# The first modulation of a two-block transformer kernel, made in eight chunks of channels

## What is computed

```
for i in range(DEPTH):
    mod = (silu_c @ ada_w[i] + ada_b[i])[:, None, :]
    mod_c = (silu_cc @ ada_w[i] + ada_b[i])[None, None, :]
    sh_m, sc_m, g_m, sh_f, sc_f, g_f = jnp.split(mod, 6, axis=-1)
    h = modulate(rmsnorm(x, norm_mix_w[i]), sh_m, sc_m)          # h * (1 + scale) + shift
    hc = modulate(rmsnorm(ctx, norm_mix_w[i]), shc_m, scc_m)
    y, y_c = ab_mixer(h, hc, ab_w_in[j], ...)                    # p = h @ w_in, 2560 columns
k = (mem @ w_k); v = (mem @ w_v)                                 # second block, needed late
```

## Time and profile before

| | us |
|---|---|
| median of 3 runs (2553.43 to 2554.41) | 2553.57 |
| the profiled execution, whole | 2553.91 |
| its span (first to last instruction) | 2552.1 |
| TensorE busy in the span | 2494.1 (98%) |
| VectorE busy | 1990.8 (78%) |
| ScalarE busy | 1175.3 (46%) |

### The profile page before, as it was taken

How to read it: one execution, slowest core, us unless ns; L and a number is a source line. 1 busy time by engine, 2 the same in 40 slices (tenths; PEclk the granted TensorE clock), 3 DMA queues, 4 the chain that set the end, 5 groups by cost and what they waited for, 6 DMA issues and landing times.

```text
span 2552.1 us, 41954 instructions
## 1 busy us (share of the span) xinstructions
PE 2494.1 (98%) x16459; PEld 2142.8 (84%) x16459; DVE 1990.8 (78%) x2455; ACT 1175.3 (46%) x1498; POOL 88.1 (3%) x116
## 2 busy tenths in 40 slices
PE   7999999999999999999999899999999999999998
PEld 5877788888889998889999688888888888888886
DVE  3876877777767886758887747888888888889887
ACT  3436200001421005531014737777777777777776
POOL 0100100000000001000002000000000000000000
PEclk9999999999999999999999999999999999999999
DMA  8843454443335454334545025999899999999996
GB/s 334 320 161 131 165 174 167 165 172 116 116 108 219 181 181 141 108 108 170 184 175 197 18 100 207 373 364 375 334 375 363 361 346 374 366 350 359 363 374 251
DMA packets 91398, 602.75 MB, mean 236 GB/s; under 512 B 9840, under 2 KB 12912, under 8 KB 24688
## 3 DMA queue, kind: packets, MB, share of 16 engines
q1 hardware_dynamic: 76848, 540.05, 56.0%
q0 software_dynamic: 14400, 60.56, 6.7%
HBM read 598.47 MB, written 2.10 MB: 235 GB/s over the span
## 4 chain that ended last, share of the span: by engine, by line
PE 92%; DVE 5%; ACT 2%; SPq 1%; issue 1%; DMA 1%; DVEq 0%; ACTq 0%
PE bank L1195 12%; PE bank L1198 12%; PE bank L1199 12%; PE bank L2546 8%; PE bank L2550 8%; PE bank L2549 8%; PE bank L2577 4%; PE bank L2581 4%; PE bank L2580 4%; PE bank L542 2%; PE bank L1432 1%; PE bank L1453 1%; PE bank L1443 1%; PE bank L2559 1%; PE bank L1244 1%; PE bank L1245 1%
## 5 line engine op out<-in xcount | busy, mean ns | idle before, releaser
L991 DVE TENSOR_TENSOR ring_part<-ring,arena_part 128x2048 fp32r<-128x2048 f32 x481 | 1080.2, 2275 | 33.1 <-ACT arena_part L1010 15.9
L2902 ACT ACTIVATE arena_part<-ring 128x2048 fp32r<-128x2048 f32 x339 | 647.7, 1920 | 191.0 <-DMA ring<-in_stream 190.1
L1195 PE MATMUL bank<-arena_part 128*128 128x256 f32 (+1 forms) x2040 | 650.3, 319 | 8.3 <-DVE ring_part L991 8.3
L1199 PE MATMUL bank<-arena_part,ring_part 128*128 128x256 f32 (+1 forms) x2040 | 646.7, 317 | 0.0
L1198 PE MATMUL bank<-h_part,arena_part 128*128 128x256 f32 (+1 forms) x1496 | 474.2, 317 | 0.0
L1195 PEld LDWEIGHTS bank<-arena_part 128*128 128x128 f32 x2040 | 388.6, 190 | 39.0 <-issue 12.6
L1199 PEld LDWEIGHTS bank<-arena_part,ring_part 128*128 128x128 f32 x2040 | 388.6, 190 | 25.7
L2546 PE MATMUL bank<-arena_part,h_part 128*128 128x512 f32 x896 | 354.1, 395 | 0.0
L2550 PE MATMUL bank<-arena_part,h_part 128*128 128x512 f32 x896 | 349.6, 390 | 0.0
L2549 PE MATMUL bank<-ring_part,h_part 128*128 128x512 f32 x896 | 348.9, 389 | 0.0
L1299 ACT ACTIVATE arena<-bank 128x256 f32<-128x256 f32 (+1 forms) x66 | 30.1, 455 | 636.7 <-PE bank L1199 635.8
(11 more groups left out here) (378 smaller groups left out, 3077.3 us busy)
## 6 DMA issues: line engine op xcount, KB each, us to landing
ring<-in_stream SPq DMA_DIRECT2D x511, 1024.0 KB, 4.9
arena<-in_ada_stream POOLq DMA_DIRECT2D x80, 512.0 KB, 4.6
consts<-in_mem_w POOLq DMA_DIRECT2D x8, 512.0 KB, 4.1
consts<-in_small POOLq DMA_DIRECT2D x1, 2800.0 KB, 11.8
arena<-in_c_rows POOLq DMA_DIRECT2D x2, 1024.0 KB, 8.3
arena<-in_ab_bias POOLq DMA_DIRECT2D x1, 2048.0 KB, 8.6
arena<-in_t_bias POOLq DMA_DIRECT2D x1, 2048.0 KB, 7.9
arena<-in_mem_t SPq DMA_DIRECT2D x1, 1024.0 KB, 5.0
```

The lines of the kernel that those rows point to most:

```text
L991: return nc.vector.tensor_tensor(low, value, high.bitcast(F32), ALU.subtract)
L1195: m = nc.tensor.matmul(out_ap, w_high, high, start=start, stop=False)
L1199: return nc.tensor.matmul(out_ap, w_low, high, start=False, stop=stop)
L2902: nc.scalar.activation(high, ring[:, where], ACT.Copy).then_inc(sem("moe_high"), 1)
```

## The change

The 2048 columns of `ada_w` now come as eight slots of their own (`ada_mix`), cut by output: slot c holds shift and scale of channel chunk c, for all input rows. They are no part of the ring's count any more and go to the ring places 0, 1, 2, 0, 1, 2, 3, 2. AB0 and AB1 are loaded ahead of them, and rounded ahead of the row copies. TensorE makes slot c in eight matmuls of 256 columns (L1958, four strips of 32 rows in PSUM), ScalarE copies the strips (L2723), two small matmuls add the strips and turn them into columns (`fold_rows`, L1968), and VectorE makes shift and scale of this chunk (`first_scale`, L3164 and L3168). The norm of chunk c, its split, and the products of AB0 and AB1 with it (`first_products`, L2002 to L2010, four banks) follow at once, while later slots of `ada_mix` still come in. SiLU of `c_rows`, the rounding of AB2 and AB3, and two of the 24 sums stand inside the loop over chunks. Memory keys and values use other banks, 18 filler matmuls stand ahead of the first value products, and GpSimd clears a buffer for the wider `silu_c`.

```diff
-START = ["K0a", "A0", "A1", "K0b", "A2", "A3", "V0a", "A4", "A5", "V0b", "A6", "A7"]
+START = ["K0a", "K0b", "V0a", "V0b"]
...
@@ TensorE
-            for k in range(2):
-                ada_products(k)
...
+            mem_key_products(range(2, 4))
+            warm(18)
+            mem_value_products()
...
+            ada_products(0)
+            ada_products(1)
             mem_value_products()
+            fold_rows(0)
             rstd_pe(bk, TT)
-            turn_rows()
-            split_products(bk, w, 4, ab_high, h_part, TT, ab_slot_high, sides=2)
+            fold_rows(1)
+            ada_products(2)
...
+            for c in range(DC):
+                if c + 3 < DC:
+                    ada_products(c + 3)
+                if c + 2 < DC:
+                    fold_rows(c + 2)
+                first_products(c)
@@ ScalarE
+            for c in range(DC):
+                for s in range(2):
+                    t = slice(SEQ * s, SEQ * (s + 1))
+                    scaled_act(bk, c == DC - 1 and s == 1, spread_last)
+                    nc.scalar.activation(ab_high[:, c, t], hv[:, c, t], ACT.Identity, bias=shift(0, 0, c, s))\
+                        .then_inc(sem("in_high"), 1)
+                if c + 3 < DC:
+                    copy_rows(c + 3)
+                if c == 1:
+                    silu_rows(rows_first, 1)
+                if c in (3, 5):
+                    slot_high_act(bk, AB_AT + 2 + (c == 5), ab_slot_high, fresh=True)
@@ VectorE
+            first_scale(0)
             spread = spread_dve(bk)
...
+            for c in range(DC):
...
+                if c + 1 < DC:
+                    first_scale(c + 1)
...
+                if c in (4, 6):
+                    slot_low_dve(bk, AB_AT + 2 + (c == 6), ab_slot_high)
+                elif c in (3, 5):
+                    if c == 3:
+                        dve.wait_ge(sem("c_rows_ready"), 1)
+                    first_chunks(c // 2 - 1, c // 2)
...
-            for n in range(2, 7):
-                first_chunks(3 * n - 6, 3 * n - 3)
+            for n, chunks in ((4, (2, 6)), (5, (6, 10)), (6, (10, 13))):
+                first_chunks(*chunks)
                 slot_low_dve(bk, AB_AT + n, ab_slot_high)
...
-            first_chunks(15, 18)
+            first_chunks(13, 15)
             slot_low_dve(bk, AB_AT + 7, ab_slot_high)
-            first_chunks(18, 21)
+            first_chunks(15, 19)
...
-            first_chunks(21, 24)
+            first_chunks(19, 22)
+            for c in range(2, 4):
+                to(kT[:, c, :])
+            slot_low_dve(bk, AB_AT + 9, ab_slot_high)
+            first_chunks(22, 24)
@@ SyncE
+            for c in range(3):
+                sp.wait_ge(sem("slots_used"), c + 2)
+                load_ada(c)
+            for c in range(3, 6):
+                sp.wait_ge(*marks["ada_made"][c - 3])
+                load_ada(c)
...
+            load_ada(6)
+            for n in range(RING, RING + 2):
+                sp.wait_ge(*marks["ada_made"][n - RING + 3])
+                load(n)
+            sp.wait_ge(*marks["ada_made"][5])
+            load_ada(7)
```

More of the change, by code:

```diff
@@ L50 @@
     ("sinks", 8), ("expert_id", EXPERTS), ("cmp_row_ok", 2),
-    ("slot_id", P), ("earlier", P), ("fold", 32),
+    ("slot_id", P), ("earlier", P),
 ]
@@ L63 @@
 LN_EVENTS = 6 * DC
-SLOTS_ADA = 16 * DC // TILES
 ADA_FIRST = [(0, n) for n in range(16, 40)]
@@ L110, in leave, with build @@
         self.i = None
-def build(nc, stream, ada_stream, mem_w, c_rows, small, x_t, ctx_t, mem_t, ab_bias, sgu, t5_bias, band_bias, cmp_bias, out):
+def build(nc, stream, ada_mix, ada_stream, mem_w, c_rows, small, x_t, ctx_t, mem_t, ab_bias, sgu, t5_bias, band_bias, cmp_bias, out):
     with ExitStack() as ctx:
@@ L1932, in _, with ada_products, fold_rows @@
             pe.wait_ge(sem("silu_c_ready"), 1)
[L1934 to L1945, removed]
-            for k in range(2):
-                ada_products(k)
             pe.wait_ge(sem("mem_split"), DC)
             mem_key_products(range(2, 4))
-            ada_products(2)
+            warm(18)
+            mem_value_products()
+            rows_copied, ada_made = [], []
+            marks["ada_made"] = ada_made
+            def ada_products(c):
+                b = bk.fill(ADA_BANKS[c % 2])
+                rows_copied.append(bk.freed(bk.turn - 1))
+                pe.wait_ge(free(b), bk.emptied())
+                at, room, landed = ada_at(c)
+                pe.wait_ge(sem(f"ada_landed{at}"), landed)
+                for late in range(2):
+                    for g in range(4):
+                        k = 4 * late + g
+                        m = nc.tensor.matmul(PS[b][32 * g:32 * g + 32, X2], silu_c[:, k, :],
+                                             room[:, k * SEQ:(k + 1) * SEQ], start=not late, stop=bool(late))
+                m.then_inc(full(b), 1)
+                ada_made.append((full(b), bk.filled()))
+            def fold_rows(c):
+                pe.wait_ge(*rows_copied[c])
+                b = bk.fill(FOLD_BANK)
+                pe.wait_ge(free(b), bk.emptied())
+                for n in range(2):
+                    m = nc.tensor.matmul(PS[b][:, 4 * c + 2 * n:4 * c + 2 * n + 2], ada_rows[c % 4][:, n * P:(n + 1) * P],
+                                         small_at("fold")[:, 0:2], start=True, stop=True)
+                m.then_inc(full(b), 1)
+            sums = bk.next_bank()
             for c in range(DC):
@@ L1955, in _ @@
             m.then_inc(full(sums), 1)
-            ada_products(3)
+            ada_products(0)
+            ada_products(1)
             mem_value_products()
+            marks["values_full"] = [(full(b), bk.filled_in[b]) for b in MEM_BANKS]
+            fold_rows(0)
             rstd_pe(bk, TT)
[L1959 to L1975, removed]
```

195 lines of the change are left out of this document (126 added, 69 removed).

## The result

The change makes the kernel slower: 2560.16 us (median of 11 executions, 2558.16 to 2562.4) against 2554.23 for the kernel before on the same chip. The ratio is 1.0025, 95% interval 1.0016 to 1.0034. That is 5.9 us, just beyond the 0.2% that a measurement of this kernel can tell. I had said 2553.7, no change. The profiled execution took 2560.99 with a span of 2559.2, against 2553.91 and 2552.1 before, so the two traces differ by 7.1 us.

A forecast was written before the change was run, and what follows sets the result against it. TensorE, busy 98% of the span, was taken as the bound, except in the first 75 us. Terms: -6.1 (Q), +4.2 (idle at the gating unit), +2.0 (clock) = +0.1, giving 2553.7 us; range 2547.3 to 2559.0.

The forecast's parts named there:

- Beginning earlier: Start of the kernel: AB0 and AB1 no longer wait behind A7, so first_products starts at about 44.0 us, against 61.73.
- The c rows: In the chunk loop: c_rows asked for at 44.8, landing 9.7 us later; SiLU ends 56.4, TensorE stands 52 to 57.3.
- The loop behind SiLU: Chunks 2 to 7: VectorE ends at 77.5 us, TensorE 2.4 later at 79.9, 6.1 us sooner than before.
- Q: Time at which AB0 and AB1 are done and L1241 begins; 86.04 us before, forecast 79.9.
- TensorE keeps up and ends 2.4 behind: End of the chunk loop: TensorE follows VectorE's end at 77.5 us by 2.4, giving 79.9.
- From Q to the gating unit: Stretch up to L1993: sgu lands at Q + 80.4, TensorE wants it at Q + 76.2, so 4.2 us idle.
- The clock: Behind the idle stretch at the gating unit the granted clock falls, costing 2.0 us; bounds 0 and 3.4.
- The rest (... the other banks, two stats areas) lies in waits. After L1993 nothing is moved.: Remaining edits, and everything behind the gating unit: no time added to the sum.
- the constants were not in time: Rival at the gating unit: constants in time, L1993 at Q + 76.2, no 4.2 and 2.0 lost; 2547.5 us, chance 0.15.
- Q was not 78: Rival: short wait for c_rows, Q = 78, or no clock fall at L1993; 2551.7 us, chance 0.28.
- the loop had one clock fall and not many: Rival in the loop: clock falls repeatedly, chunks 2 to 7 take 5.4 to 7.8 us each; 2568 us, chance 0.04.
- the third rival: In the loop: c_rows come behind five stream slots, 15.0 us instead of 9.7, Q = 85.2; 2559.0 us, chance 0.11.

The follow-up runs named there:

- short filler: Changed kernel with 10 filler matmuls ahead of the third chunk's products in the loop, where TensorE stood waiting; +4.7 us over the kernel before.
- 3: Changed kernel with the gating unit's table asked for early, in the middle of the chunks, not after the 24th sum; +1.8 us over the kernel before.
- 5: Changed kernel with SiLU at the last chunk, the loop's sums behind the loop and GpSimd's queue held back to the sixth ada_products; +3.7 us over before.
- 1: Changed kernel with two bank turns skipped on three engines between the loop and the token products; +4.0 us over the kernel before.
- 2: Kernel before with only its bank rotation moved on by six (two back) behind the first modulation; +5.1 us over the kernel before.
- 8: Changed kernel with the gating unit's table early and two bank turns skipped just ahead of the layer norm near 1085 us; -3.8 us against before.
- 7: Changed kernel with 5, 3 and the skip of 1 together; -5.3 us against the kernel before.
- 9: Changed kernel with 5, 3 and the skip of 8 together; 2545.37 us, -8.1 us against the kernel before.
- first filler kernel of experiment 6: Changed kernel with 19 filler matmuls ahead of TensorE's wait for the gating unit's table; +10.3 us over the kernel before.
- third group: Last of three groups, each on one chip, in which the twelve follow-up kernels ran; the kernel before took 2553.42 us beside it.

## Why the prediction was wrong

By its steps:

- **Beginning earlier**: right. `first_products` starts at 45.1 for 44.0.
- **The c rows**: right. Asked for at 45.9 for 44.8, 9.9 us for 9.7, SiLU done at 57.8 for 56.4, TensorE idle until 58.6 for 57.3. ScalarE's row is the one forecast:

```profile
55.86 1.91 ACT L2740 ACTIVATE arena<-arena 128x2048 f32<-128x2048 f32 x1 [4.95 <-DMA arena<-in_c_rows]
```

- **The loop behind SiLU**: mis-sized. Q is 83.5 for 79.9. Of the 3.6, 1.3 is the later SiLU. The rest is the step "TensorE keeps up and ends 2.4 behind", which took the clock fall in the loop as free. TensorE does end 2.4 behind VectorE's last low part (81.1), but it did not keep up: the products of chunk 2 took 5.3 us at half the clock, for 2.9 in the chunks beside it. The next strip copy waited for them, and behind it in ScalarE's queue stand the rounding of AB2 and the shifts of chunk 4, which VectorE needs. So chunk 4 took 7.5 us on VectorE, where the sum had 5.1:

```profile
65.04 0.38 ACT L2723 ACTIVATE arena<-bank 128x256 f32<-128x256 f32 x1 [4.54 <-PE bank L1958]
65.32 1.91 ACT L1017 ACTIVATE arena_part<-ring 128x2048 fp32r<-128x2048 f32 x1
67.12 0.89 ACT L2746 ACTIVATE arena_part<-h_normed,mod 128x256 fp32r<-128x256 f32 x2
```

  The short filler gives 2.25 of it back.
- **From Q to the gating unit**: right, with the 4.9 idle us for the 4.2 forecast, released by `sgu`, at Q + 81.2 for Q + 80.4. VectorE's last sum ended at 160.1, Q + 76.7 for Q + 75.8; of the 0.9 more, 0.6 is a wait at 147.5 for a chunk of weights, which my chain did not have. A longer wait of this kind, 4.5 us at 92.5, cost nothing, since VectorE had to wait for ScalarE's high part of AB6 all the same (until 118.8). That the table alone is the reason is shown by 3, and that it hangs on TensorE's progress by 5.
- **The clock**: right, 2.4 us for 2.0.
- **"The rest (... the other banks, two stats areas) lies in waits. After L1993 nothing is moved."** This is the step that failed. No instruction was moved, but from Q to the cross attention near 1110 every bank of the rotation was. That cost 5.7 us near 1110 and gave back 1.4 near 1040 (experiments 1, 2 and 8). The listing with bank numbers, made from the two kernels alone, shows it.

So the start came to +4.9 at the attention, where the sum had +0.1: 3.6 at Q, 0.9 from Q to the gating unit, 0.4 of clock. That alone would have been 2558.5, inside my range. In the traces the banks added 4.3 to it, and the clock near 1500 took 2.9 away; the median lies at 2560.2, outside. Of the rivals none happened: the constants were not in time, Q was not 78 and the clock did fall at L2035, the c rows did not wait behind the five slots, and the loop had one clock fall and not many, although that one cost 2.3 us. The time agrees best with the third rival's 2559.0, but that is luck: by its reason the c rows would have taken 15 us, and they took 9.9.

## What to carry to other kernels

An edit that changes how many turns are drawn from a shared rotation (banks, buffers, semaphores) edits the program as far as the next place that sets the rotation, here 1000 us on: list who shares a bank with whom up to there, above all where the rotation is aligned or where a copy stands behind other work. When a wait is taken away, ask what the queue behind it holds; here the wait for one transfer hid that the stream was late in any case. And a table that is needed at a fixed point of TensorE's work should be asked for by that work, not by the end of another engine's chain.

## What the runs showed that I had not expected

The clock fall near 1500 us, behind an idle stretch of 3.1 us that the traces of before and of the change both have, comes and goes. Its mean clock from 1490 to 1510 is 0.83 before the change and in 3, and 1.00 in the changed kernel and in 8:

```profile
1490.00:1510.00 20.00, 16.93 (x138) 14.46 (x137) 6.60 (x18) 5.23 (x12) 0.00 (x0) 0.83 0.19 57
```

```profile
1490.00:1510.00 20.00, 16.93 (x271) 15.29 (x270) 8.84 (x24) 7.37 (x19) 0.00 (x0) 1.00 0.28 98
```

It is worth 2.9 us, half of what the change costs. It is not the only place of this kind. Between 640 and 700 us six of the fourteen traces lose 1.5 us or more to it, and those of before and of the change none. In 2, 7, 8 and 9 this is near 650 us, behind an idle stretch of 1.79 us that all fourteen have. In both kernels with the filler at the gating unit it is from 680 to 700 us (granted clock 0.91), where TensorE has no idle stretch; eight small products (32 x 512, 3.69 us) stand ahead of the fall. In the first filler kernel of experiment 6 the collision at 1110 cost its wait of 3.84 us, but the pair of products behind it took 7.17 us and not 8.86. In the same way TensorE's stops of 1.46 and 2.89 us at the last piece of `ada_mix` went without and with a fall.

One trace of each kernel does not tell whether a fall belongs to the kernel or to the execution. The executions of one kernel tell a part of it. The kernel before ran 27 times beside the third group: 7 times with a mean granted clock of 0.994 over the whole span, in 2551.2 us on average, 16 times with 0.993, in 2553.3, and 4 times with 0.992, in 2555.0. So the falls do vary between executions of one kernel, by about as much as the change costs. At which places they vary is not shown, and 2 to 3 us of each difference between two profiled executions stay open with it. The banks are not the cause near 1500: from 1110 us on TensorE's products and their banks are the same in both kernels.
